# Two-slot weight transfers, earlier cached keys, a token-row router and an fp32 gather in a hybrid decoder step

## The reference

```
x = x + token_mixer(rms_norm(x), S0, ...)          # o_t = S_t^T q_t; the sample sequences read a given state S0
x = x + cross_attention(rms_norm(x), mem_k, mem_v) # sample: cached keys and values, one pair per sequence
h = rms_norm(x) * norm_ffn_g
logits = h @ w_router + b_router
top_v, top_e = top_k(logits, 4);  gates = softmax(top_v)
for every expert e and its tokens:
    glu, lin = split(h[tokens] @ w1[e] + b1[e])
    act = min(glu, 7) * sigmoid(1.702 * min(glu, 7)) * (clip(lin, -7, 7) + 1)
    x[tokens] += gate * (act @ w2[e] + b2[e])
y = rms_norm(x)
```

## Time and profile before

| | |
|---|---|
| time, median of 3 runs | 1312.46 us (1311.49 to 1313.07) |
| the profiled execution, own time | 1314.39 us |
| its span, first to last instruction | 1312.7 us |
| mean granted TensorE clock | 0.982 of full speed |
| TensorE (PE) busy | 1197.4 us, 91% |
| VectorE (DVE) busy | 404.3 us, 31% |
| ScalarE (ACT) busy | 228.8 us, 17% |
| mean DMA rate over the span | 356 GB/s |

### The profile page before, as it was taken

How to read it: one execution, slowest core, us unless ns; L and a number is a source line. 1 busy time by engine, 2 the same in 40 slices (tenths; PEclk the granted TensorE clock), 3 DMA queues, 4 the chain that set the end, 5 groups by cost and what they waited for, 6 DMA issues and landing times.

```text
span 1312.7 us, 17381 instructions
## 1 busy us (share of the span) xinstructions
PE 1197.4 (91%) x6756; PEld 593.6 (45%) x6756; DVE 404.3 (31%) x815; ACT 228.8 (17%) x356; POOL 56.6 (4%) x81
## 2 busy tenths in 40 slices
PE   7999999879499999999999998999989999989995
PEld 5778899657243443433433232323333232323231
DVE  3555667526712222121321212120312212121203
ACT  4332144312310111111111111101111011111012
POOL 5202001010300000000000000000000000000000
PEclk9999999989699999999999999999999999999998
DMA  9732289794599999999999999999999999999993
GB/s 314 250 120 83 97 262 309 253 380 163 232 373 418 418 417 417 417 417 417 419 418 418 418 417 419 417 417 417 417 417 419 418 418 418 418 418 418 417 417 119
DMA packets 123893, 467.06 MB, mean 356 GB/s; under 512 B 7440, under 2 KB 54064, under 8 KB 90864
## 3 DMA queue, kind: packets, MB, share of 16 engines
q1 hardware_dynamic: 116848, 455.37, 87.3%
q0 software_dynamic: 1616, 6.65, 1.6%
q10 hardware_dynamic: 5392, 4.54, 1.1%
HBM read 460.84 MB, written 5.70 MB: 355 GB/s over the span
## 4 chain that ended last, share of the span: by engine, by line
PE 49%; DMA 36%; SPq 9%; DVE 3%; issue 2%; ACT 1%; DVEq 0%; ACTq 0%
DMA ring<-w 34%; PE bank L1624 15%; PE bank L1276 9%; SPq L303 7%; PE bank L1656 6%; PE bank L1443 5%; PE bank L1600 4%; PE bank L1580 2%; PE bank L1431 2%; SPq L305 1%; DMA ring<-k_t 1%; DMA ring<-v_c 1%; PE bank L1643 1%; DMA ring<-w_in 1%; PE bank L1476 1%
## 5 line engine op out<-in xcount | busy, mean ns | idle before, releaser
L1624 PE MATMUL bank<-ring,rest 128*64 128x512 f32 x2048 | 463.6, 596 | 29.8 <-DMA ring<-w 27.5
L1624 PEld LDWEIGHTS bank<-ring,rest 128*64 128x64 f32 x2048 | 139.4, 136 | 333.9 <-issue 234.7
L1656 PE MATMUL bank<-ring,rest 128*64 128x512 f32 x1024 | 226.8, 595 | 16.4 <-ACT rest L731 16.4
L1212 DVE TENSOR_SCALAR rest<-bank 128x512 f32<-128x512 f32 x32 | 22.1, 691 | 521.7 <-PE bank L1624 521.7
L1656 PEld LDWEIGHTS bank<-ring,rest 128*64 128x64 f32 x1024 | 70.8, 137 | 151.8 <-issue 127.8
L1191 DVE TENSOR_TENSOR rest<-rest,bank 128x512 f32<-128x512 f32 (+1 forms) x102 | 66.9, 680 | 227.6 <-PE bank L1600 227.5
L1276 PE MATMUL bank<-rest,ring 128*128 128x288 f32 (+1 forms) x512 | 124.6, 403 | 8.7 <-DMA ring<-w_in 8.7
L1276 PEld LDWEIGHTS bank<-rest,ring 128*128 128x128 f32 x512 | 97.7, 192 | 33.1 <-DMA ring<-w_in 8.7
L727 ACT ACTIVATE rest<-rest 128x512 f32<-128x512 f32 x32 | 20.2, 630 | 520.7 <-DVE rest L1212 520.7
L1600 PE MATMUL bank<-rest 128*128 128x512 f32 (+1 forms) x204 | 98.4, 611 | 1.3 <-ACT rest L739 1.3
L1443 PE MATMUL bank<-split 128*128 128x288 f32 x576 | 81.2, 302 | 2.0 <-DVE split L1058 1.8
(11 more groups left out here) (297 smaller groups left out, 699.8 us busy)
## 6 DMA issues: line engine op xcount, KB each, us to landing
ring<-w SPq DMA_DIRECT2D x384, 1024.0 KB, 21.8
ring<-w_in SPq DMA_DIRECT2D x12, 1024.0 KB, 12.0
ring<-k_t SPq DMA_DIRECT2D x8, 1024.0 KB, 6.2
ring<-v_c SPq DMA_DIRECT2D x8, 1024.0 KB, 13.1
ring<-w_xk SPq DMA_DIRECT2D x4, 1024.0 KB, 5.0
ring<-w_xv SPq DMA_DIRECT2D x4, 1024.0 KB, 5.0
ring<-w_out SPq DMA_DIRECT2D x4, 1024.0 KB, 6.6
ring<-w_xq SPq DMA_DIRECT2D x4, 1024.0 KB, 6.2
```

The source lines that it names most:

```text
L1624: last = t.matmul(out, slots[:, k, :], w[:, col], start=False, stop=(k == KT - 1))
L1656: last = t.matmul(ps[2][CAP * ds:CAP * ds + CAP, :], actT[:, a * P + CAP * cg:a * P + CAP * cg + CAP], w[:, cg, 512 * ds:512 * ds + 512], ...
```

## The change

1. The transfer of expert weights takes two neighbouring slots (2 MB) in one DMA. In each partition it brings two consecutive rows of w1 or four of w2, 16 KB in one piece. So the row that a partition holds is another one, and the other operand is permuted to match: the gather takes every second column of the token rows (`cols_d`), and the transposes of the activation take every fourth column (`act[:, a:512:4]`). SP and TensorE wait once for two units.
2. Five cached keys go to slots 11 to 15 as soon as the mixer's scratch is free; the other keys, the values and `w_xo` go round in the freed slots, and `w_xo` comes last. The splits of `w_xo` into upper and lower parts (`upper_unit`, `lower_part`) are issued later.
3. The router has tokens on partitions (three matmuls of 32 columns for each chunk), so that the logits need no copy and no transposes. The sum of squares is taken from squares of `xT` (ACT), added up by POOL and multiplied by ones on TensorE. The token rows are scaled by 1/rms alone; the gain `ffn_g` is multiplied in when the gather is copied out (`gain_k`).
4. The gather is one fp32 matmul instead of three bf16 ones; ACT copies its first bank out, DVE the second. `sel` is made by one instruction instead of six. The choice of experts uses `match_replace` instead of indices and comparisons.
5. In the state reads the head is the inner loop.

```diff
+            both = cells(s * SLOT, (s + 2) * SLOT)
             if q < W1_UNITS:
-                return eng.dma_start(slot[s], w1[e, q * P:(q + 1) * P, :]).then_inc(ring_in[s], 16)
+                src = w1[e, q * P:(q + 2) * P, :].rearrange("(p r) c -> p (r c)", r=2)
+            else:
+                src = w2[e, (q - W1_UNITS) * 256:(q - W1_UNITS + 2) * 256, :].rearrange("(p r) c -> p (r c)", r=4)
+            return eng.dma_start(both, src).then_inc(ring_in[s], 16)
...
-            return u % PRE if u < U_XO else PRE + HELD + u - U_XO
+            if u < U_KC:
+                return u % PRE
+            if u < U_KC + EARLY:
+                return SLOTS - EARLY + u - U_KC
+            if u < U_XO - EARLY:
+                return (u - EARLY) % PRE
+            if u < U_XO:
+                return SLOTS - EARLY + u - (U_XO - EARLY)
+            return (U_KC + u - U_XO) % PRE
...
+                for j in range(first, BODY * EXP_UNITS, 2):
+                    sp.wait_ge(units_used, g * (BODY * EXP_UNITS) + j + 1 - SLOTS + 1)
+                    load_expert_units(sp, i * BODY, j)
...
+            for k in range(KT):
+                act_e.wait_ge(x_add, KT + k + 1)
+                a.activation(sq_r[:, k, :], xT[:, k, :], ACT.Square).then_inc(rsq_done, 1)
...
+                a.activation(h_rows[0:R, tt, 512:1024], ps[Y_BANK[TT + tt]][0:R, :], ACT.Copy,
+                             scale=yrs[0:R, tt:tt + 1]).then_inc(h_ready, 1)
...
+                for k in range(KT // 2):
+                    last = a.activation(xg[parity][:, k, :], ps[4][:, k * P:(k + 1) * P], ACT.Copy, scale=gain_k[:, k:k + 1])
...
-                for b in range(DECB):
-                    last = t.matmul(out, q2m[:, h, b * TS:(b + 1) * TS], st[:, b, h, :], start=False, stop=(b == DECB - 1))
+            for b in range(DECB):
+                for h in range(H):
+                    last = t.matmul(outs[h], q2m[:, h, b * TS:(b + 1) * TS], st[:, b, h, :], start=False, stop=(b == DECB - 1))
...
-                return t.matmul(ps[6][0:NE, 0:T], wr[:, k, :], xT[:, k, :], start=(k == 0), stop=(k == KT - 1))
+                for tt in range(TT):
+                    R = ROWS[tt]
+                    last = t.matmul(ps[L_BANK[tt]][0:R, 0:NE], xT[:, k, tt * P:tt * P + R], wr[:, k, :],
+                                    start=(k == 0), stop=(k == KT - 1))
...
+                    cols_d = slice(256 * (d // 2) + d % 2, 256 * (d // 2) + 256, 2)
                     for tt in range(TT):
-                        for s in range(3):
-                            last = t.matmul(ps[4 + d // 4][:, (d % 4) * P:(d % 4 + 1) * P],
-                                            hx[:, s, tt, d * P:(d + 1) * P], sel[:, tt, :],
-                                            start=(tt == 0 and s == 0), stop=(tt == TT - 1 and s == 2))
+                        R = ROWS[tt]
+                        last = t.matmul(ps[4 + d // 4][:, (d % 4) * P:(d % 4 + 1) * P],
+                                        h_rows[0:R, tt, cols_d], sel[0:R, tt, :], start=(tt == 0), stop=(tt == TT - 1))
...
-                        last = t.transpose(ps[4][:, a * P:(a + 1) * P], act[:, a * P:(a + 1) * P], ident)
+                        last = t.transpose(ps[4][:, a * P:(a + 1) * P], act[:, a:512:4], ident)
```

More of the change, by code:

```diff
@@ L64 @@
 UPD_BANK = [4, 5, 6, 3]
[L65 removed]
+Y_BANK = [3, 4, 3, 2, 1, 3]
+L_BANK = [5, 6, 7]
+PADS = 4
+LOWEST = -3.0e38
 GM_BANK = [7, 4, 3]
@@ L221, in hybrid_decoder_step @@
         selG = m(10752, 384, TT, P)
-        sel = m(11136, 192).bitcast(BF16).rearrange("p (t s) -> p t s", t=TT)
+        sel = m(3072, TT * P, TT, P)
+        gate = m(3456, TT * NE, TT, NE)
         oh = [m(11328 + 32 * i, 32).bitcast(BF16) for i in range(2)]
@@ L348, in load_unit @@
                              ).then_inc(ring_in[unit_slot(u)], 16)
-            for u in range(U_XO):
+            for u in range(U_KC):
                 if u >= PRE:
@@ L678, in _ @@
                 a.copy(oT[:, c, 0:SEQ], ps[c % 3][:, 0:SEQ]).then_inc(pv_done_a, 1)
+            for i in (12, 13, 14):
+                upper_unit(i)
             act_e.wait_ge(kv_used, 2 * DECB)
             a.copy(o_x, ps[4][:, 0:MEM]).then_inc(ox_done, 1)
-            upper_unit(15)
             a.activation(srn, eps, ACT.Sqrt).then_inc(act_step, 1)
-            for n in range(2 * TT):
-                half, tt = n // TT, n % TT
-                R = ROWS[tt]
-                act_e.wait_ge(y_ev, n + 1)
-                a.activation(junk[0:R, half, tt, :], y[0:R, tt, 512 * half:512 * half + 512], ACT.Square,
-                             accum_out=ysq[0:R, half, tt:tt + 1]).then_inc(y_sq, 1)
@@ L700, in _ @@
+            act_e.wait_ge(rss_ps, 1)
+            act_e.wait_ge(act_step, 2)
+            for tt in range(TT):
+                R = ROWS[tt]
+                a.activation(yrs[0:R, tt:tt + 1], ps[L_BANK[tt]][0:R, NE:NE + 1], ACT.Sqrt, bias=eps[0:R],
+                             scale=1.0 / D).then_inc(y_std, 1)
+            act_e.wait_ge(yrs_done, 1)
+            act_e.wait_ge(y_ev, TT)
             for tt in range(TT):
-                act_e.wait_ge(h_tok, tt + 1)
-                act_e.wait_ge(hx_zero, 1)
@@ L1077, in split_bias, with x_rows @@
                     v.memset(selGT, 0.0).then_inc(selgt_zero, 1)
-            def x_rows(half):
-                for tt in range(TT):
-                    dve.wait_ge(y_ps, TT * half + tt + 1)
+            def x_rows(pieces):
+                for n in pieces:
+                    half, tt = n // TT, n % TT
+                    dve.wait_ge(y_ps, n + 1)
+                    if half:
+                        dve.wait_ge(h_ready, tt + 1)
                     v.tensor_copy(y[0:ROWS[tt], tt, 512 * half:512 * half + 512],
-                                  ps[Y_BANK[TT * half + tt]][0:ROWS[tt], :]).then_inc(y_ev, 1)
+                                  ps[Y_BANK[n]][0:ROWS[tt], :]).then_inc(y_ev, 1)
             for c in range(KT):
@@ L1553, in _ @@
                 if c == 5:
-                    x_rows(0)
+                    x_rows(range(2))
+                if c == 6:
+                    x_rows(range(2, TT))
             router(KT - 2)
-            router(KT - 1).then_inc(lg_ps, 1)
-            x_rows(1)
-            pe.wait_ge(lg_done, 1)
-            pe.wait_ge(y_ev, TT)
+            router(KT - 1)
+            pe.wait_ge(rsq_done, KT)
+            pe.wait_ge(rsq_sum, KT - 2)
             for tt in range(TT):
                 R = ROWS[tt]
-                last = t.transpose(ps[5][0:R, tt * NE:(tt + 1) * NE], std[0:NE, tt * P:tt * P + R], ident[0:NE, 0:NE])
-            last.then_inc(lt_ps, 1)
+                for k in (0, KT - 1):
+                    last = t.matmul(ps[L_BANK[tt]][0:R, NE:NE + 1], sq_r[:, k, tt * P:tt * P + R], ones[:, 0:1],
+                                    start=(k == 0), stop=(k == KT - 1))
+            last.then_inc(rss_ps, 1)
+            x_rows(range(TT, 2 * TT))
             pe.wait_ge(chosen_done, 1)
```

270 lines of the change are left out of this document (123 added, 147 removed).

## The result

The changed kernel takes 1327.6 us (median of 4 runs, 1325.5 to 1330.5), the kernel before 1312.7: 1.0117 times as long, 95% interval 1.0095 to 1.0138. The forecast was 1263, with 0.92 on faster. The change made the kernel 15 us (1.2%) slower, and the time lies outside the range. The profiled execution took 1330.5 us, its span 1328.8.

What follows compares the result with a forecast made beforehand. It took expert-weight transfers as the bound after PE's lead ran out, plus the head before the experts. Savings 20 + 3.8 + 8.7 + 17 = 49.5 us from 1314.4 gave 1264.9, median 1263; range 1250 to 1288.

Steps and rivals of the forecast that it cites:

- signs that it named for being wrong: Rate staying at 422 GB/s, PE without DMA wait in the last experts, or ACT's splits between values and projection.
- The fp32 gather: Gather on PE: 48 instructions at 0.115 us, 5.5 us; a pair of experts 56.4 us, hidden below the transfers.
- the cover of 12 us: In the experts, PE at 903 us stays 12 us below the stream's 915, 0.4 us an expert.
- The two-slot transfers: Expert weights in 16 KB pieces: 2.44 us a unit, 430 GB/s; 22 us net saved, counted as 20.
- no gain over 8 KB pieces: First rival, expert transfers: a unit stays 2.485 us, 5.7 us saved instead of 20, total 1277; chance 0.15.
- State reads, keys, values: Head: state reads 3.0 us, 3.8 saved; keys and values 7.2 us each, 9.7 saved, net 8.7.
- just at the limit: Head: `w_xo` blocks and ACT's third split barely ready by the end of the values; 1 us given back (0 to 4).
- fourth rival: Head: early keys fail, `w_xo` or `w_out` late, splits hold up projection; 8.7 and more lost, 1272 to 1278; chance 0.07.
- Router to first expert: Last residual to first w1 matmul: 13.7 us instead of 31.6; 17.9 saved, counted as 17 for the clock.
- the term for the clock: Router to first expert: lower PE clock may take some back; saving cut from 17.9 to 17, or 12.4 at half speed.
- third rival: Gather's stepped weight loads take twice as long: gather 11.0 us, a pair 62, total 1343; chance 0.06.
- point of decision: Third rival turns the sign once experts take 29.5 us more: pair 60.4, gather 9.5 us, 0.2 us an instruction.

Runs made afterwards that it cites:

- e6: Changed kernel with the third token tile gathered with all 128 rows, its 96 empty rows zeroed by GpSimd; step of two kept; 1279.2 us.
- e8: Changed kernel with 128 rows in the third token tile, token rows written for stepless weight loads, and two queue moves in the head; 1266.9 us.
- e1: Changed kernel with ScalarE writing token rows in the order the gather loads them, so its weight loads have no step; 1321.9 us.
- e9: Kernel of e8 with w1's two-slot transfers bringing 8 KB pieces instead of 16 KB; w2 stays at 16 KB; 1276.4 us.
- e10: Changed kernel with only the five early keys issued behind the last w_out block instead of ahead of it; one run, 1322.8 us.
- e5: Changed kernel with the 32-row token tile first in every second block of columns, so 8 changes of rows a gather instead of 16; 1297.9 us.
- e7: Kernel before with its bf16 gather taking the third token tile with 32 rows in place of 128; one run, 1328.5 us.

## Why the prediction was wrong

The forecast for the profiled execution was 1264.9 us, and it took 1330.5: 65.6 too much. The experts hold 960.7 - 917.5 = 43.2 of it, the stretch up to the projection 13.0, the stretch from the router to the first expert 9.6. Two of the signs that it named for being wrong came: PE is the bound to the end, and ACT's splits stand between the values and the projection.

**The fp32 gather: the step that failed.** It said "48 x 0.115 = 5.5 us" and drew 0.115 from the earlier trace rows. The duration was right for what those rows show: all 24 of their instructions have 128 rows. e6, where the gather has only such tiles, takes 5.85 us with the step of two, and e8 5.55 without. But the instructions of the gather were counted and not looked at one after the other: by taking 32 rows in the third token tile the change removes a padding, and so adds 16 changes of rows. They cost 2.9 of the 3.25 us by which the gather was too long, and the step of two the other 0.3. The working looked for a danger only in the step and priced it from nothing to 5.5 us; the edit with the price stood in the same line of the diff. A pair on PE became 59.87 instead of 56.4, more than the transfers' 58.73, and the cover of 12 us on which the forecast rested was gone.

The Trainium skill says, on the page "TensorEngine Tiling (Array Packing)", section Key Properties, that changing the tiling mode, as opposed to the tile, drains TensorE. That rule was not weighed. It speaks against this change if a plain matmul with 32 rows counts as another mode, which no run shows by itself; the trace fits it: the idle 0.12 us of the weight loads in e1 stand exactly at the changes.

The rule that was weighed, of the Trainium skill's page "SBUF — State Buffer" (Specifications (TRN2)), makes a step of two free and a step of four not. The runs show 0.006 us an instruction for two, and for the four transposes 0.09 us on 0.66 together; so the first is nearly free, and the second costs far less than double.

**The two-slot transfers.** Right: 2.447 us a unit for 2.44, 428 GB/s for 430, and 918.1 us of experts in e6 for 917.5. That the experts came out to within 1 us is in part luck: the working had 22 us net and counted 20. In the kernel after none of it shows, because PE is the bound. The rival "no gain over 8 KB pieces" fell by e9.

**State reads, keys, values.** Their own terms were right or cautious: 2.1 us for 3.0, 7.1 for 7.2. The failing step was the next one: "PE needs them more than 20 us later, so nothing is charged", for what is late behind the five keys. The last `w_out` block landed at 198.06 and its split came next in ACT's and DVE's queues, so PE stood still and the projection after it began late; e10 gives 6.5 us back. And `w_xo` was not "just at the limit", 1 us, but the third split ended some 8 us after the values' last matmul. That is the fourth rival, and its price of 8.7 and a few more was right: 13.0 in all, the 3.8 of the state reads with them.

**Router to first expert.** Forecast 13.7 us from the last residual to the first w1, or 14.6 with what was kept back for the clock; measured 348.08 - 323.90 = 24.2. Up to the gather it was 7.4 of 7.3: the new router does what was worked out. The first gather then took 15.03 where 5.5 and 0.9 for the clock were allowed: 8.75 is its length at 2.4 GHz, with the changes of rows, and 6.3 more come from the lower clock; the products behind it lose another 0.8. Between 326 and 347 us the granted clock is 0.52 in after and 0.76 in e6, where the first gather takes 8.52. So the term for the clock was under-priced too.

**The sign.** The third rival named the right place, the gather, with the wrong cause: the step that it feared costs 0.3 us. Its point of decision, a gather of 9.5 us, was worked out for a head that brings 29.5 us, and without the first gather's own growth. The head brought 7, so that 8.75 was enough. What the third rival feared for the gather's time and what the fourth feared for the head came together, and the range, which left the third out, had no room for that. With the rows padded, the step taken out and the queues mended, the kernel takes 1266.9 us, 4 us above the forecast, and its first w1 starts at 328.19, where "near 325" was forecast. Within these few us the terms for the transfers, the state reads, the keys and values and the new router stood.

## What to carry to other kernels

When a matmul replaces others, write its instructions down in order and compare neighbours: the same number of rows or not, and whether the old code padded for it. Zeros in 96 rows cost nothing here, a tile of 32 rows between tiles of 128 cost twice 0.18 us. When loads are moved ahead in a queue, ask what stands behind them there and in the queue of the engine that prepares them, not only when the last consumer needs it; a copy that the critical engine waits for goes ahead of preparatory work that can wait.

## What was not expected of the hardware

- A change between 128 and 32 rows costs 0.17 to 0.19 us in fp32 (e5, e6) and 0.097 in bf16 (e7), because the next weights are not loaded beside the running matmul.
- The more changes of rows the first gather has, the longer it runs at 1.2 GHz. Between 326 and 347 us the granted clock is 0.52 with 16 changes (after), 0.67 with 8 (e5) and 0.76 with none (e6), behind the same pauses of PE; that gather takes 15.03, 12.22 and 8.52 us. All six kernels with 16 changes in the fp32 gather have 13.4 to 15.0 us there, the three with none 5.6 to 8.5. Why is not shown.
- In e7 the clock fell to 1.2 GHz in most pairs although PE was busy 97% of the time; in after, with as many changes, it fell once in all pairs. So changes of rows alone do not bring it about.
- fp32 weight loads with a step of two take 0.006 us more of 0.11; DVE reading both inputs with a step of four takes 1.07 instead of 0.69 us.
- One core draws 428 GB/s with 16 KB pieces (e8) and 424 with w1 in 8 KB and w2 in 16 KB pieces (e9); the kernel before has 422 where 8 KB pieces and 407 where 4 KB pieces are in flight. So the 11 ns a piece worked out from 4 and 8 KB became (2.485 - 2.447) / 4 = 9.5 ns between 8 and 16.
